# Prompt attention's query tiles 2 and 3 moved into the decode-attention loop

## The reference, cut to what matters

```
# A, 4 heads, each with two 64-wide halves c = 0, 1 (causal for the prompt)
s = einsum('bqhcd,bkhcd->bchqk', q, k) * 64 ** -0.5
p = masked_softmax(s, k_pos <= q_pos)
o = einsum('bhqk,bkhv->bqhv', p[:, 0] - lam * p[:, 1], v)
# B, 4 query heads on one key/value head of 128: compressed blocks (o_cmp),
# selected blocks (o_sel) and a window of 512 positions (o_win)
```

## Time and profile before

| | us |
|---|---|
| median of 3 runs (1862.41 to 1870.23) | 1865.84 |
| the profiled execution | 1861.1 |
| its span, first to last instruction | 1859.3 |
| PE busy | 1632.8 (88%) |
| DVE, ACT, POOL busy | 811.1, 587.3, 111.7 |
| bytes moved | 375.37 MB, 202 GB/s over the span |

### The profile page before, as it was taken

One profiled execution on the slowest core, in us unless ns is written; L12 is line 12 of the kernel. 1 busy time (PEld: TensorE's weight loads), 2 busy tenths in 40 slices (PEclk: granted clock), 3 DMA queues, 4 the chain that ended last, 5 costly groups with the idle time before them and its releaser, 6 DMA issues. The chain is left out here.

```text
span 1859.3 us, 38873 instructions
## 1 busy us (share of the span) xinstructions
PE 1632.8 (88%) x14817; PEld 1266.4 (68%) x14817; DVE 811.1 (44%) x1592; ACT 587.3 (32%) x1353; POOL 111.7 (6%) x168
## 2 busy tenths in 40 slices
PE   6999999998998899989968987888888888279998
PEld 5888888786777767767656765666666666067776
DVE  4212222253256444344337553456655556374221
ACT  4311212322122232321125224454555545252110
POOL 3000000061000010000020000000000000120000
PEclk9999999999999999999978888999999999589999
DMA  7565655785332424251455308999999997392443
GB/s 204 169 189 178 195 175 163 234 271 180 109 105 93 120 92 143 97 155 49 114 213 170 115 37 294 363 378 376 380 393 380 381 367 300 107 317 71 138 141 118
DMA packets 218728, 375.37 MB, mean 202 GB/s; under 512 B 41990, under 2 KB 122359, under 8 KB 217231
## 3 DMA queue, kind: packets, MB, share of 16 engines
q1 hardware_dynamic: 215006, 361.35, 57.0%
q0 software_dynamic: 3248, 9.44, 1.5%
q10 hardware_dynamic: 288, 2.10, 0.3%
HBM read 336.37 MB, written 40.71 MB: 203 GB/s over the span
## 5 line engine op out<-in xcount | busy, mean ns | idle before, releaser
L369 PE MATMUL pj_ps<-pj_whi,pj_xhi 128*128 128x512 f32 (+1 forms) x1024 | 413.8, 404 | 6.1 <-PEq L86 6.0
L370 PE MATMUL pj_ps<-pj_wlo,pj_xhi 128*128 128x512 f32 (+1 forms) x1024 | 399.4, 390 | 0.0
L371 PE MATMUL pj_ps<-pj_whi,pj_xlo 128*128 128x512 f32 (+1 forms) x1024 | 398.2, 389 | 0.0
L287 DVE TENSOR_TENSOR pj_wlo<-pj_w,pj_whi 128x1024 fp32r<-128x1024 f32 (+1 forms) x128 | 157.0, 1227 | 454.1 <-ACT pj_whi L245 452.7
L245 ACT ACTIVATE pj_whi<-pj_w 128x1024 fp32r<-128x1024 f32 (+1 forms) x128 | 132.3, 1034 | 507.1 <-DMA pj_w<-in_w_in 505.5
L369 PEld LDWEIGHTS pj_ps<-pj_whi,pj_xhi 128*128 128x128 f32 x1024 | 195.8, 191 | 65.9 <-issue 29.5
L371 PEld LDWEIGHTS pj_ps<-pj_whi,pj_xlo 128*128 128x128 f32 x1024 | 196.1, 192 | 40.3
L370 PEld LDWEIGHTS pj_ps<-pj_wlo,pj_xhi 128*128 128x128 f32 x1024 | 196.4, 192 | 33.8
L1588 ACT ACTIVATE da_kT<-da_tp 128x512 f32<-128x512 f32 x200 | 119.3, 597 | 166.5 <-PE da_tp L1469 154.2
L1675 DVE COPY da_kT<-da_tp 128x512 f32<-128x512 f32 x128 | 88.6, 692 | 72.0 <-PE da_tp L1469 71.7
L3117 PE MATMUL ou_ps<-ou_whi,ou_mhi 128*128 128x512 f32 x256 | 104.6, 409 | 6.3 <-DVE ou_wlo L3041 6.3
(11 more groups left out here) (523 smaller groups left out, 2221.0 us busy)
## 6 DMA issues: line engine op xcount, KB each, us to landing
at_early_a<-in_cache_a_kv SPq DMA_DIRECT2D x128, 512.0 KB, 6.6
da_pa<-in_cache_a_kv SPq DMA_DIRECT2D x128, 512.0 KB, 7.0
pj_w<-in_w_in SPq DMA_DIRECT2D x120, 512.0 KB, 4.6
px_pages<-in_cache_b_kv SPq DMA_DIRECT2D x256, 128.0 KB, 2.6
at_early_b<-in_cache_b_kv SPq DMA_DIRECT2D x128, 128.0 KB, 6.6
da_pb<-in_cache_b_kv SPq DMA_DIRECT2D x128, 128.0 KB, 7.3
ou_w<-in_w_out SPq DMA_DIRECT2D x32, 512.0 KB, 4.2
proj<-pj_out SPq DMA_DIRECT2D x52, 256.0 KB, 4.6
```

What stands on the lines that cost most here:

```text
L287: dve.tensor_tensor(self.wlo[:, r, :, 0:n], self.w[:, r, :, 0:n], self.whi[:, r, :, 0:n], ALU.subtract).then_inc(self.wlo_ready, 1)
L369: pe.matmul(acc, hi, high, start=kc == 0, stop=False)
L370: pe.matmul(acc, hi, low, start=False, stop=False)
L371: last = pe.matmul(acc, lo, high, start=False, stop=kc == KC - 1)
```

## The change

`prompt_attend` keeps query tiles 0 and 1 (`EARLY_T = 2`): 32 units and 24 value steps. All five row tiles are turned there, earlier in the loop (at i = 0, 2, 4, 6, 8), and the guest `Blocks` starts at i = 9. The value columns go to a buffer that outlives the stage (`k.vals`), by DMA for group A and by 10 POOL copies for B; each row tile is therefore loaded with three DMAs and stored with one more. The 8 copies of `b_win` to the window state, one per section before, are issued together after the last section. The loads of page groups 0 and 1 are issued at sections 2 and 3 of 6.

Tiles 2 and 3 are a guest of `decode_attend`, `LateTiles`, from n = 2: per unit two iterations, n = 2 to 70 in all. It has one bank each for scores, transposes and output. To free three banks, decode gives up one `sa`, the bank `pt` (the probabilities now take their turn in the two `tp` banks) and `ptb` (it shares a bank with `sb`). `kT` and `pw` become single buffers. The two halves of a group A head are scored one at a time, in different iterations. The six section stores of 256 KB are issued from POOL.

```diff
+AV = 512
+EARLY_T = 2
 # prompt_attend
-    TURN_AT = {0: (0,), 3: (1,), 8: (2,), 12: (3,), 15: (4,)}
-    GUEST_FROM = 16
+    TURN_AT = {0: (0,), 2: (1,), 4: (2,), 6: (3,), 8: (4,)}
+    GUEST_FROM = 9
...
+class LateTiles:
+    FROM = 2
...
+    def steps(self):
+        for at in range(2 * self.NU + 5):
+            u, odd = divmod(at, 2)
+            yield (u if not odd and u < self.NU else None,
+                   self.of.get(u - 1) if odd else None,
+                   self.of.get(u - 2) if not odd else None,
+                   self.of.get(u) if odd else None,
+                   self.of.get(u - 2) if odd else None)
...
+        for s_, t_, v_, _, _ in self.steps():     # PE
+            if s_ is not None:
+                score(s_)          # waits for exped >= u
+            if t_ is not None:
+                turn(t_)           # waits for weighed or exped, copied >= i
+            yield
+            if v_ is not None:
+                attend(v_)         # waits for copied >= i + 1
+            yield
...
+        for s_, t_, _, _, _ in self.steps():      # ACT
+            if s_ is not None:
+                exp(s_)            # waits for maxed >= u + 1
+            if t_ is not None:
+                copy(t_)           # waits for turned >= i + 1
+            yield
...
+        for s_, _, _, w_, f_ in self.steps():     # DVE
+            if s_ is not None:
+                row_max(s_)
+            if w_ is not None and self.pvs[w_][2] == 0:
+                weigh(w_)
+            if f_ is not None and self.pvs[f_][3] == 3:
+                finish(f_)
+            yield
...
 # decode_attend, PE
                     for x in range(min(2, own)):
                         turn(n, x)
+                    if n >= guest.FROM:
+                        next(tiles, None)
                     if n >= 2:
                         turn_p(n - 2)
-                    for x in range(2, own):
+                    for x in range(2, min(3, own)):
+                        turn(n, x)
+                    if n >= guest.FROM:
+                        next(tiles, None)
+                    for x in range(3, own):
                         turn(n, x)
                     if n >= 2:
                         values(n - 2)
+                for _ in tiles:
+                    pass
...
-        sa = [s.ps(f"sa{i}", [P, 512]) for i in range(2)]
-        sbp = s.ps("sb", [P, 512])
-        pt = s.ps("pt", [P, 4, P])
-        ptb = s.ps("ptb", [P, 512])
+        sa = s.ps("sa", [P, 512])
+        sb_bank = s.ps("sb", [P, 512])
+        sbp, ptb = sb_bank[:, 0:P], sb_bank[:, P:3 * P]
+        gs, gt, go = s.ps("gs", [P, 512]), s.ps("gt", [P, 4, P]), s.ps("go", [P, 4, HEAD])
...
-                        if a >= 2:
-                            pe.wait_ge(exped_a, a - 1)
+                        if a:
+                            pe.wait_ge(exped_a, a)
...
                     pe.wait_ge(exped_b, n + 1)
-                    pe.wait_ge(pb_copied, n)
+                    pe.wait_ge(biased, min(n + 2, N))
+                    if n:
+                        pe.wait_ge(pb_copied, n)
```

More of the change, by code:

```diff
@@ L1060, in prompt_attend @@
         po = [s.ps(f"po{i}", [P, 4, HEAD]) for i in range(2)]
-        one = s.sb("one", [P, P], F32R)
-        late = s.sb("late", [P, P], F32R)
+        one, late = k.one, k.after
         blocks = Blocks(nc, d, k, s)
@@ L1084, in prompt_attend, with a_values @@
         c_made = s.sem("c_made")
-        NA = [sum(1 for v in pvs[:i] if v[2] == 0) for i in range(NV + 1)]
+        NA = [sum(1 for v in pvs[:i] if v[2] == 0) for i in range(NPV + 1)]
         def tile(t):
             return k.rows_p[:, t, :] if t < PT else k.rows_s[:, :]
+        def a_values(t):
+            return k.vals[:, t, 0:AV] if t < PT else k.vals_s[:, 0:AV]
         with nc.Block() as block:
@@ L1163, in score @@
                         kn = P // len(pair)
-                        pe.matmul(scores[x % 3][:, 0:n], k.attT[p0:p0 + kn, qc, P * t:P * t + P],
-                                  k.attT[p0:p0 + kn, kc, 0:n], start=True, stop=False)
+                        pe.matmul(scores[x % 3][:, 0:n], k.queries(qc, t)[p0:p0 + kn, :],
+                                  k.keys(kc)[p0:p0 + kn, 0:n], start=True, stop=False)
                     for x in pair:
@@ L1265, in weigh @@
                     if i >= 2 and a >= 2:
-                        j = next(x for x in range(NV) if NA[x] == a - 2 and pvs[x][2] == 0)
+                        j = next(x for x in range(NPV) if NA[x] == a - 2 and pvs[x][2] == 0)
                         dve.wait_ge(turned, j + 1)
@@ L1302, in _ @@
                 done = 0
-                for i in range(NV + 3):
-                    if i < NV:
+                for i in range(NPV + 3):
+                    if i < NPV:
                         while done <= min(pvs[i][0] + 1, NU - 1):
@@ L1346, in decode_attend @@
     a_of = {n: a for a, n in enumerate(a_steps)}
+    tp_order = []
+    for n in range(N + 2):
+        own = [("key", n, x) for x in range(len(jobs[n]))] if n < N else []
+        tp_order += own[0:2]
+        if n >= 2 and n - 2 in a_of:
+            tp_order.append(("p", n - 2, 0))
+        tp_order += own[2:]
+    tp_at = {job: i for i, job in enumerate(tp_order)}
     with Stage(nc, "da") as s:
@@ L1447, in _, with bank_free @@
                 sp.wait_ge(stored, 16 * 3 * HA)
+            @block.gpsimd
+            def _(pool):
+                guest.pool(pool)
             @block.tensor
             def _(pe):
+                def bank_free(job):
+                    i = tp_at[job]
+                    if i < 2:
+                        return
+                    kind, n, x = tp_order[i - 2]
+                    before = tp_order[:i - 1]
+                    if kind == "p":
+                        pe.wait_ge(pa_copied, a_of[n] + 1)
+                    elif jobs[n][x] % 2 == 0:
+                        pe.wait_ge(act_copied, sum(1 for y in before if y[0] == "key" and jobs[y[1]][y[2]] % 2 == 0))
+                    else:
+                        pe.wait_ge(dve_copied, sum(1 for y in before if y[0] == "key" and jobs[y[1]][y[2]] % 2 == 1))
                 def turn(n, x):
@@ L1567, in _ @@
                 for x in range(2):
-                    pe.matmul(sa[x][0:4 * HA, :], both[:], oa[:, 4 * x:4 * x + 4, :], start=True,
+                    pe.matmul((sa, gs)[x][0:4 * HA, :], both[:], oa[:, 4 * x:4 * x + 4, :], start=True,
                               stop=True).then_inc(gathered, 1)
@@ L1598, in softmax @@
                         width = 512 if what == "page" else NS
-                        act.activation(e[:, a % 2, 0:width], sa[a % 2][:] if what == "page" else sn[:, b % 2, :], ACT.Exp,
+                        act.activation(e[:, a % 2, 0:width], sa[:] if what == "page" else sn[:, b % 2, :], ACT.Exp,
                                        bias=nm[:, b % 2, c:c + 1], accum_out=l[:, b % 2, c:c + 1]).then_inc(exped_a, 1)
@@ L1640, in _ @@
                 act.wait_ge(consts_ready, 1)
+                tiles = guest.act(act)
                 for n in range(N + 9):
@@ L1774, in _ @@
                 dve.sem_inc(consts_ready, 1)
+                tiles = guest.dve(dve)
                 for n in range(N + 10):
@@ L3228, in build @@
 def build(nc, a, o):
-    d, k = Names(), Names()
+    d, k = Names(), Kept()
     d.x_prompt = a["x_prompt"][0]
```

353 lines of the change are left out of this document (257 added, 96 removed).

## The result

| | before | after |
|---|---|---|
| median of 4 runs each, us | 1866.02 (1862.41 to 1870.23) | 1846.33 (1842.86 to 1849.62) |
| ratio, 95% interval | | 0.9883 (0.986 to 0.9905) |
| median of 5 further runs of after (15 of before) | 1865.08 | 1839.62, ratio 0.9856 (0.9835 to 0.9878) |
| span of the profiled execution | 1859.3 | 1841.1 |

The ratio is worked out from all runs and not from the two medians, whose quotients are 0.9894 and 0.9863. The change makes the kernel 20 to 25 us faster, 1.1 to 1.4%. The forecast was 1820 us, 2.5% faster: the sign was right and the time lies in the range, but less than half of the forecast gain of 46 us came in the first measurement.

The account below looks back on a forecast made before the run. Decode was taken as close to two limits, page-data DMA and PE's in-order chain. From 1861.1 us, 68 saved in `prompt_attend` and 22 added in decode gave 1815; the median, 4.7 above, gave 1820 us, range 1796 to 1850.

Parts of the forecast that it names:

- the waits for page data "near zero": Decode: PE's weight loads would hardly wait for page data any more, where they waited 3.8 us per ten-iteration period.
- 37 us of streams left over: Decode: the moved tiles stream 54 us, of which 17 fall into existing waits, leaving 37.
- 16 of new waits: Decode: 12 us of lateness plus 4 for DVE's `weigh` meeting long parts of `finish`; between 0 and 40.
- shared banks: Decode: probabilities' transposes wait for key copy 0 in the `tp` banks; costed at nothing, 36 us without covers.
- Lateness: Decode: ACT's guest exponential waits for DVE's row maximum behind `finish`, delaying key copy 0 and PE; 12 us.
- half a pair: Decode: low end pricing a 64-row group A score at half a two-score pair, 0.57 us; 6 us off the streaming.
- What the holes absorbed: Decode: guest work filling PE's waits, 11 us before key transposes and 6 us before values, 17 together.
- The late beats: End of `prompt_attend`: beats 20 to 27 without a host, about 2.9 us per prompt tile, 12 us for four.
- the bound of the changed kernel (1802): Rival: DMA still bounds decode, the guest falls wholly into holes, decode grows only 4 us; 1802 us, chance 0.2.
- The exposed beats: Rival: beats of `Blocks` left exposed in `prompt_attend` cost the low bound, 50 us saved; 1838 us, chance 0.15.
- The lock chain: Rival: single and shared banks lock PE, ACT and DVE into one chain, decode +99 us; 1897 us, chance 0.1.
- The fourth: Rival: decode stretches by most of what is saved, so little changes; 1855 to 1875 us, chance 0.05.

Follow-up runs that it names:

- e3: Kernel before, with page loads after the first four groups cut to an eighth of the columns: decode 435.1 us.
- e9: Kernel before, with the step for new keys moved to seventh place in the order: ratio 0.9957, decode 458.1 us.
- e1: Changed kernel, with the step for new keys moved to seventh place, so page loads are evenly spaced: ratio 0.979, decode 489.1 us.
- e5: Changed kernel without the attention of tiles 2 and 3, page loads after the first four groups cut to an eighth: decode 458.6 us.
- e14: Changed kernel without tiles 2 and 3, with short page loads, and a bank of their own for the turned probabilities: decode 434.8 us.
- e15: Changed kernel with short page loads and the guest's first beat behind the probabilities' transposes instead of ahead: decode 501.8 us.
- e8: Changed kernel with DVE's guest step ahead of the part of `finish` instead of behind it: ratio 0.9842, decode 497.5 us.
- e18: Changed kernel with even order, spread `b_win` copies, DVE's guest step first, and full-height (128-row) guest scores for group A: ratio 0.9764, decode 483.7 us.
- e6: Changed kernel with the eight `b_win` copies issued two at a time behind the first four sections: ratio 0.9839, decode 502.0 us.
- e2: Changed kernel, with page loads after the first four groups cut to an eighth of the columns: decode 484.6 us.

## Why the prediction was wrong in size

- **Decode: the waits for page data "near zero".** This is the step that failed, and its 20 us are the largest error. The sum took PE's chain as 52.9 us a period, all 3.8 us of the earlier trace rows removed eight times, 30 us, because a longer chain would make the transfers the faster side. The chain did come out right (53.2 us a period in `e3`), but only 10 of some 28 us of waits vanished (462.7 - 435.1 before, 501.9 - 484.6 after), not 30. I had read every wait at `at_early_a` as a matter of rate, since the DMA share was 0.98 to 1.02. The rows held a sign against it: two buffers hold the ring's four groups, and in the earlier trace rows the waits stand at one of them alone. In the kernel before `e9` shows that the rate did set the sum. Once the rate no longer did, the distance of four steps was next, as `e1` shows.
- **Decode: what the tiles add.** 37 us of streams left over and 16 of new waits, 53; measured 49.5. The parts: shared banks, forecast nothing, bound 36; measured 23.5 uncovered and 6 as the kernel stands (`e5`, `e14`, `e15`). Lateness, forecast 12, measured 5 (`e8`); the 4 for `weigh` was not tried by itself. The 64-row scores, priced like those of 128 rows, took 1.22 and 1.00 us in place of 0.92 and 0.71, 4.8 us in all (`e18`). My low end for them, half a pair, had the wrong sign. The Trainium skill ("TensorEngine Tiling (Array Packing)", Key Properties) says that a change of tiling mode drains the engine. The rows of `e18` and the 0.54 us wait above fit this, though no run tells a drain from another cause of the wait; I had not brought it to the sum. The sentence that the prediction takes from the Trainium skill ("TensorE: Matmul & The Clock Gate"), that a matmul of few rows takes as long as a full one, stands in that page's table "Why this matters for your kernels" and not in Part 3; here the 64-row score took 0.30 us more. What the holes absorbed must then be some 20 us by difference and not 17; PE's waits for ACT's key copy in the key transposes (L1469 before, L1701 after) went from 26.2 to 11.7 us. That these errors cancel to 3.5 us is luck.
- **`prompt_attend`: 57 saved and not 68.** Beats 8 to 18 ended where the sum had them. The late beats, forecast 12 us, took 20.4: 4 to 5 are the copies of `b_win` in front of the stores (`e6`), which the change issues in one piece at just that time. In `e6` the four tiles take 14.8 us; what is over 12 there goes with the lower clock, which the prediction had among its bounds and not in its sum, and whose share wasn't tried by itself. That bound was added up wrongly: twice 2.9 us for each of four tiles is 11.6 more and not 8, so the low end was 46 and not 50. The exit took 4.6 (1056.2 to 1060.8) in place of 3.3. Two executions of the changed kernel differ by 4 us in this stage (118.5 and 114.4), so part of the 11 us may be chance.
- **Rivals.** The DMA did not stay the bound of the changed kernel (1802): its share is 0.91, and fewer bytes gain only the 17 us of waits. The exposed beats (1838) came true in part. The lock chain (1897) did not: the banks cost 6 us with the beats in place; but `e15` shows that one line's place decides over 17. (Its sum of 553 counts the 40 for lateness once, where the text says twice.) The fourth, that decode stretches by most of what is saved, is near in kind: decode took back 40 of the 57 us, though the time stayed under its 1855.
- **What the profile was to show.** Decode's start within its bracket (1060.8); late tiles 3 us apart at first; clock 0.98; what follows decode unchanged: all as said. Window loads 59 to 60 us apart while the guest runs: 60 to 68. DMA share 0.93 to 0.95: 0.91 over decode. Waits near zero: no.

## What to carry to other kernels

When a change lengthens the chain beside a stream of loads, the waits for data don't vanish by themselves: for each buffer of the ring, count the steps between the one that frees it and the one that needs it, and hold that time against a load's issue to landing; a DMA share near 1 hides the shortest of these distances until the rate is no longer the limit. An order of steps that makes all distances equal cost nothing here and gave 12 to 17 us, beside the 20 to 25 of the whole change. And transfers without a deadline are put where nobody waits for the queue or the end of a stage: the same eight copies cost 4 to 5 us in front of small stores and 13 to 14 at a barrier.

## What the runs showed of the hardware that was not expected

- A 128-row weight load behind a 64-row matmul was not overlapped: it waited 0.54 us (384 columns), and the score with its mask took 1.22 us (512 columns) where the full-height one took 0.92.
- Full transfers did not slow the engines' own work: with an eighth of the bytes (DMA share 0.24 in `e2`) decode took 484.6 us, with all of them 501.9 and 503.4, which is 486.2 and 484.9 less the waits for pages.
- Eight copies of 508 KB between DRAM tensors, issued by SP in one piece, held up four stores of 256 KB that POOL issued behind them: these took 6.3 us to land (median) and 2.4 with the copies spread (`e6`).
- Between short groups with waits for DVE the granted clock was at its lower level (0.51), and the same eight matmuls went from 1.15 to 2.07 us; from 1010.0 to 1020.4 it was as low with PE busy for all 10.4 us.
